# Layer norms: GpSimd centres and weights half of each row

## What is computed

```python
def layer_norm(x, g, b):
    xf = x.astype(jnp.float32)
    mu = jnp.mean(xf, -1, keepdims=True)
    var = jnp.mean(jnp.square(xf - mu), -1, keepdims=True)
    y = (xf - mu) * lax.rsqrt(var + LN_EPS)
    return (y * g.astype(jnp.float32) + b.astype(jnp.float32)).astype(x.dtype)
...
    for l in range(DEPTH):
        x = layer_norm(alpha * x + 0.5 * swiglu(x, ffn_w_gate[l, 0], ffn_w_up[l, 0], ffn_w_down[l, 0]),
                       ln_g[l, 0], ln_b[l, 0])
...
```

## Time and profile before

| | us |
|---|---|
| median of 3 runs | 1566.58 |
| the 3 runs, lowest to highest | 1566.1 to 1567.77 |
| span of the profiled execution | 1564.4 |
| TensorE busy | 1550.8 (99%) |
| VectorE busy | 1054.8 (67%) |
| ScalarE busy | 771.3 (49%) |
| GpSimd busy | 35.5 (2%) |

### The profile page before, as it was taken

One profiled execution on the slowest core, in us unless ns is written; L12 is line 12 of the kernel. 1 busy time (PEld: TensorE's weight loads), 2 busy tenths in 40 slices (PEclk: granted clock), 3 DMA queues, 4 the chain that ended last, 5 costly groups with the idle time before them and its releaser, 6 DMA issues.

```text
span 1564.4 us, 20746 instructions
## 1 busy us (share of the span) xinstructions
PE 1550.8 (99%) x8610; PEld 1340.2 (86%) x8610; DVE 1054.8 (67%) x1290; ACT 771.3 (49%) x917; POOL 35.5 (2%) x86
## 2 busy tenths in 40 slices
PE   9999999999999999999999999999999999999998
PEld 9888888899888888888898888888888898888886
DVE  7866657768675666655777665576555778965556
ACT  5735434567353444445455354455454465454543
POOL 2000000000000000000100000010000100000000
PEclk9999999999999999999999999999999999999999
DMA  9365554743565656556463665547555573375551
GB/s 282 123 216 188 189 190 160 242 162 109 176 205 192 195 174 217 188 191 194 161 216 126 219 191 192 192 148 242 190 189 191 160 211 100 130 242 189 189 189 52
DMA packets 198357, 285.98 MB, mean 183 GB/s; under 512 B 9199, under 2 KB 166967, under 8 KB 198263
## 3 DMA queue, kind: packets, MB, share of 16 engines
q1 hardware_dynamic: 194663, 272.19, 53.4%
q0 software_dynamic: 3456, 11.94, 2.3%
q10 hardware_dynamic: 144, 0.52, 0.1%
HBM read 283.58 MB, written 1.05 MB: 182 GB/s over the span
## 4 chain that ended last, share of the span: by engine, by line
PE 95%; DVE 3%; ACT 1%; issue 1%; DMA 0%; DVEq 0%; ACTq 0%
PE ps L438 50%; PE ps L467 25%; PE ps L471 13%; PE ps L490 3%; DVE wlo L299 1%; PE ps L1652 1%; PE ps L1964 0%; ACT whi L288 0%; PE ps L1456 0%; DVE arena L2174 0%; PE ps L1644 0%; DMA x<-in_x 0%; DVE small L940 0%; DVE x L566 0%; PE ps L1131 0%
## 5 line engine op out<-in xcount | busy, mean ns | idle before, releaser
L299 DVE TENSOR_TENSOR wlo<-raw,whi 128x2048 fp32r<-128x2048 f32 (+3 forms) x254 | 567.0, 2262 | 219.8 <-ACT whi L288 219.1
L288 ACT ACTIVATE whi<-raw 128x2048 fp32r<-128x2048 f32 (+3 forms) x260 | 479.8, 1882 | 18.9 <-DMA raw<-in_w_out 4.9
L438 PE MATMUL ps<-whi,yt 128*128 128x512 f32 (+1 forms) x1472 | 460.9, 386 | 0.5 <-DVE wlo L299 0.5
L467 PE MATMUL ps<-xt,whi 128*128 128x512 f32 x1728 | 432.4, 392 | 0.0
L467 PEld LDWEIGHTS ps<-xt,whi 128*128 128x128 f32 x1728 | 314.1, 189 | 59.1
L438 PEld LDWEIGHTS ps<-whi,yt 128*128 128x128 f32 x1472 | 274.8, 188 | 54.8 <-DVE wlo L299 0.9
L438 PE MATMUL ps<-wlo,yt 128*128 128x512 f32 (+1 forms) x736 | 283.7, 385 | 0.0
L471 PEld LDWEIGHTS ps<-xt,wlo 128*128 128x128 f32 x1728 | 235.7, 190 | 16.9
L471 PE MATMUL ps<-xt,wlo 128*128 128x256 f32 x1728 | 240.9, 282 | 0.0
L438 PE MATMUL ps<-whi,xt 128*128 128x512 f32 (+4 forms) x778 | 219.0, 359 | 0.8 <-issue 0.3
L777 ACT ACTIVATE arena<-ps 128x512 f32<-128x512 f32 x108 | 64.1, 593 | 280.5 <-PE ps L471 280.5
(11 more groups left out here) (242 smaller groups left out, 958.6 us busy)
## 6 DMA issues: line engine op xcount, KB each, us to landing
raw<-in_ffn_w_up SPq DMA_DIRECT2D x76, 1024.0 KB, 5.3
raw<-in_ffn_w_down SPq DMA_DIRECT2D x76, 1024.0 KB, 4.9
raw<-in_ffn_w_gate SPq DMA_DIRECT2D x44, 1024.0 KB, 5.3
raw<-in_diff_w_qkv SPq DMA_DIRECT2D x12, 1024.0 KB, 5.0
raw<-in_w_in_conv SPq DMA_DIRECT2D x10, 1024.0 KB, 5.0
raw<-in_w_out SPq DMA_DIRECT2D x8, 1024.0 KB, 4.9
raw<-in_w_in_mlstm SPq DMA_DIRECT2D x7, 1024.0 KB, 8.0
raw<-in_w_in_mlstm SPq DMA_DIRECT2D x8, 768.0 KB, 4.2
```

The source lines that it names most:

```text
L288: nc.scalar.activation(whi[:, u.slot, 0:u.size], raw[:, u.slot, 0:u.size], ACT.Copy).then_inc(w_hi[u.slot], 1)
L299: nc.vector.tensor_tensor(wlo[:, u.slot, 0:u.size], raw[:, u.slot, 0:u.size], whi[:, u.slot, 0:u.size].bitcast(F32), ALU.subtract).then_in ...
L438: m = nc.tensor.matmul(out_, p, q, start=first and n == 0, stop=last and n == 2, skip_group_check=True)
L467: nc.tensor.matmul(o.rearrange("p (a n) -> p a n", a=2), parts[c][0], xt2[:, :, c, :], start=c == 0, stop=False, skip_group_check=True)
```

## The change

In each norm and row tile, GpSimd now does the centring of columns 512 to 1023 in two instructions: `tensor_scalar` subtracts the mean (it waits for `ln_var`), and `tensor_tensor` multiplies by the gain (it waits for the first, by a new semaphore `ln_centred`). VectorE keeps the centring of columns 0 to 511, the root and both scalings; ahead of the second scaling it waits for `ln_centred`. GpSimd's loop over the norms now also covers norm 9, without a load behind it.

```diff
@@ ln_normal (VectorE)
-            def centre(h):
-                half = slice(h * 512, h * 512 + 512)
-                link.mark(nc.vector.scalar_tensor_tensor(
-                    out=res[:, t, half], in0=res[:, t, half], scalar=mv[:, t, 0:1],
-                    in1=gb[:, 0, half], op0=ALU.subtract, op1=ALU.mult))
+            half = slice(0, 512)
...
-            centre(0)
+            link.mark(nc.vector.scalar_tensor_tensor(
+                out=res[:, t, half], in0=res[:, t, half], scalar=mv[:, t, 0:1],
+                in1=gb[:, 0, half], op0=ALU.subtract, op1=ALU.mult))
             dve.wait_ge(ln_sd, TT * n + t + 1)
...
             scale(0)
-            centre(1)
+            dve.wait_ge(ln_centred, 2 * (TT * n + t) + 2)
             scale(1)
@@ ln_gpsimd
-            pool.wait_ge(ln_x, 4 * (n + 1))
-            load_gb(pool, n + 1)
+            half = slice(512, 1024)
+            for t in range(TT):
+                if t == 0:
+                    pool.wait_ge(gb_loaded, 32 * (n + 1))
+                pool.wait_ge(ln_var, TT * n + t + 1)
+                nc.gpsimd.tensor_scalar(res[:, t, half], res[:, t, half], mv[:, t, 0:1], None,
+                                        ALU.subtract).then_inc(ln_centred, 1)
+                pool.wait_ge(ln_centred, 2 * (TT * n + t) + 1)
+                nc.gpsimd.tensor_tensor(res[:, t, half], res[:, t, half], gb[:, 0, half],
+                                        ALU.mult).then_inc(ln_centred, 1)
+            if n < N_LN - 1:
+                pool.wait_ge(ln_x, 4 * (n + 1))
+                load_gb(pool, n + 1)
```

More of the change, by code:

```diff
@@ L374, in build @@
         ln_sd = sem("ln_sd")
+        ln_centred = sem("ln_centred")
         sd = sb("sd", [P, TT])
@@ L2545, in _ @@
                 .then_inc(mem_loaded, 16)
-            for n in range(N_LN - 1):
+            for n in range(N_LN):
                 for f in ffns:
-                    if f.gated and FFN_LN[f.k] + 1 == n:
+                    if f.gated and FFN_LN[f.k] + 1 == n < N_LN - 1:
                         split_lo_gpsimd(pool, order[f.tail[0].index + 4])
```

## The result

The changed kernel takes 1573.68 us (median of 5 runs, 1573.4 to 1575.31), the kernel before 1566.55 (median of 5, 1566.1 to 1567.77). The ratio is 1.0048, with a 95% interval of 1.0038 to 1.0059: 7.1 us slower, where 10 were forecast.

A forecast was written before the change was run, and what follows sets the result against it. TensorE was taken as the bound, waiting on VectorE's scalings. Delays of 8.7 (first scalings), 0.6 (norms 7 and 9) and 0.9 (first row tiles) sum to 10.2 us, giving 1577 from 1566.6; range 1568 to 1585.

The forecast's parts named there:

- the forecast case: Whole kernel: GpSimd's multiplication holds the first scaling, making the time 1574 to 1580 us; chance 0.45.
- The main mechanism: In each norm, GpSimd's multiplication takes the shared ports ahead of the first scaling, which ends 1.09 us late.
- the first scaling keeps its 0.75 us: Sign that the prediction is wrong: the first scaling's row stays at 0.75 us instead of reading 1.4 to 1.7.
- the second of the prediction's steps: Length of GpSimd's subtraction of the mean: 0.50 us after the centring, ending 1.24 after the centring's start.
- The next step: GpSimd's multiplication takes the ports at about 1.54 us after the centring's start and keeps them 1.12, until 2.66.
- the first scaling wins the race: Rival: the first scaling gets the ports before GpSimd's multiplication; +1 to +4 us, 1568 to 1570; chance 0.17.
- The rival of a slower GpSimd: GpSimd's subtraction takes 1.12 us instead of 0.50, 8 us more, 1590; chance 0.27 together with small instructions held.
- 8 x 1.09 = 8.7: Second row tile of norms 0 to 6 and 8: TensorE waits 1.09 us longer for the first scaling, 8.7 us.
- 5 x 0.31 = 1.5: Second scaling 0.31 us late in five places: norms 7 and 9, and first row tiles of norms 4, 6, 8.
- The rival of no collision: VectorE and GpSimd overlap on these operands; the second scaling starts earlier, -1.4 us, 1565.2; chance 0.08.
- the second rival: VectorE's small instructions (L573, L575) are held by GpSimd too; 1582 us; chance 0.27 together with a slower GpSimd.
- The estimate from the Trainium skill's GPSIMD Engine Reference (§3.1): GpSimd's one-input loop of 512 elements priced at 768 ns, 0.27 us more per place, 3.5 us more, 1580.

The follow-up runs named there:

- run 1: The kernel before, with 22 scratch instructions for GpSimd alone (subtractions and multiplications) between 40 and 80 us; 1569.06 us in its only timed run.
- Run 10: The changed kernel with GpSimd's subtraction over 64 columns instead of 512, the multiplication still over 512; 1574.02 us.
- run 9: The changed kernel with the second row tile put back on VectorE, GpSimd doing the first row tile alone; 1568.35 us.
- run 3: The changed kernel without GpSimd's subtraction and its wait, so that GpSimd only multiplies; 1574.04 us.
- run 5: The changed kernel with VectorE's centring of columns 0 to 511 taking its second tensor from PSUM, not the gain from SBUF; 1570.18 us.
- run 6: The changed kernel with L572 and L574 written as operations of one tensor and two per-row numbers; 1574.10 us.
- run 4: The changed kernel without GpSimd's multiplication, so that GpSimd only subtracts; 1567.47 us.
- run 7: The changed kernel with GpSimd on columns 768 to 1023 alone, VectorE centring 512 to 767 between its two scalings; 1567.93 us.
- run 2: The changed kernel with a constant, 0.25, in place of the mean in GpSimd's subtraction; 1572.66 us.
- run 8: The changed kernel with GpSimd released by the mean and not by the variance, 0.25 us earlier; 1573.03 us.

## Why the prediction was right, and where it was not

The direction and the place held. TensorE is the bound, what counts most is the two scalings of the second row tile, and shared ports put GpSimd behind the centring. The time lay 3.3 us under the point and inside the range, just below the forecast case (1574 to 1580).

The main mechanism did not hold. The prediction named its own sign of being wrong, that "the first scaling keeps its 0.75 us", and it does. Of its other signs, L593 ended 1.44 us after the centring and not 0.5, and VectorE's idle for `ln_centred` is 1.22 us and not near zero. The waits of L490 did grow to "13 or more" (13.8), but not by 1.4 each: they are more waits, for both scalings. That the time still came out near the forecast is in part luck, as the sum below shows.

The step that failed is the length of GpSimd's subtraction, the second of the prediction's steps: "It ends at 1.24. As bounds I take 0.50 and 1.12". The subtraction ended at 2.18, 1.44 after the centring. The row used, a selection over 512 columns (`sel` in the earlier trace rows), is a different operation, and on 4 partitions; run 1 measured 1.56 us for this one. The upper bound, 1.12, was a two-input instruction's time, and run 1 shows that the one-input instruction takes longer, 1.56 against 1.27. What the estimate of 0.50 did describe is how long it holds the ports: L572 ended at 1.31, forecast "about 1.3".

The next step fell with it: "it takes the ports at about 1.24 + 0.3 = 1.54". The multiplication was issued at 2.26, after the first scaling had begun at 1.61. So the rival "the first scaling wins the race" is what happened, but not by the race of 0.1 to 0.3 us that I described, and not at its price. It gave 0.2 to 0.4 for the second scaling; the chain that is 0.9 longer makes it 0.76. Run 10, with a shorter subtraction, shows the collision that was forecast, at 1574, where it was priced at 1577: its scalings ended 2.97 and about 3.6 after the start, where 3.21 and 3.88 were forecast. The rival of a slower GpSimd had a longer subtraction add 8 us more (1590). It takes the collision with the first scaling away instead: with 512 columns the time is 1573.7, with 64 it is 1574.0.

The terms of the sum: 8 x 1.09 = 8.7 for the first scaling became 8 places of 0.49 on average, 3.9, paid for the second scaling less what TensorE had to spare. The 5 x 0.31 = 1.5 for the second scaling in norms 7 and 9 and in the first row tiles of 4, 6 and 8 became 0.77 + 0.7 + 2.1 = 3.6. The five places were the right ones (run 9: 2.1 us for the three first row tiles). So a term that was 4.8 too high and one that was 2.1 too low partly cancelled, which is luck.

The rival of no collision (-1.4) is excluded by runs 3 and 5. The small instructions are held too, as the second rival supposed: 0.24 us in the changed kernel, 0.84 in run 3. It was L572 that was hit, by the subtraction, and that cost nothing (run 6).

The rule of the Trainium skill (SBUF — State Buffer, "Who interferes with whom") speaks of the whole instruction. Run 3 agrees for the multiplication (L572 ended 0.02 after it); for the subtraction the measurement differs, since L572 and most of the first scaling (its first 0.57 us of 0.75) ran while it was still under way. The estimate from the Trainium skill's GPSIMD Engine Reference (§3.1), 768 ns, lay nearer than 0.50 and was still half of what was measured.

No run is faster than the kernel before; runs 4 and 7 show why. By the prediction's reading the gain to be had is 0.7 us in two places, and in each variant here GpSimd's instructions hold, or are held by, one of the two scalings or a centring.

## What to carry to other kernels

Moving half of an engine's work to an idle engine can pay only if the new chain, with its hand-overs, ends before the old one would have, and holds nothing on the path meanwhile: here 0.74 us of VectorE's time became 1.56 + 1.27 us on GpSimd, without collisions. Take the price of an instruction from a row of the same operation or measure it alone; a row of a like one missed by a factor of three. And ask of a shared port how long each side holds it: in every row here a VectorE instruction with two SBUF inputs and a GpSimd instruction with two finish one behind the other, and dividing such work between the two engines gained nothing at 256 columns (run 7) and lost at 512.

## What was not expected of the hardware

- GpSimd's subtraction of one number for each row takes 1.56 us over 512 columns, its multiplication of two tensors 1.27; over 256 columns 0.92.
- The one-input instruction lets VectorE go well before its end. L572 ends 0.57 us after the centring, the subtraction over 512 columns 1.44 after it; over 256 columns (run 7) it is 0.35 and 0.79. The two-input one holds VectorE to its end (run 3).
- GpSimd's multiplication also holds a VectorE instruction with one tensor in SBUF, L991 in run 1: 1.44 us in place of 0.35.
- With the number in SBUF the subtraction seems to come to the ports twice. The one at 46.87 in run 1 began under a split of VectorE that ended at 48.04, did not delay the next (2.28 us), and ended 1.35 after that one. With a constant, L572 is held 0.09 us less (run 2). That the first visit is for the number is inferred from these two, not shown.
- When GpSimd's subtraction started 0.01 us ahead of the centring (run 8, second row tiles), the centring still took its 0.74 us. L573, the small instruction, then took 0.37 us, as with the constant, and the subtraction ended 0.09 earlier than in the changed kernel. That would fit a first visit made ahead of the centring; it is not shown either.
- At the start of the changed kernel's execution GpSimd's `sel`, which took 0.63 us in the earlier trace rows, took 1.45, beside a split that began 0.01 us earlier; it ends 0.50 after it. Timeline of GpSimd, then VectorE:

```profile
10.13 1.45 POOL L2388 TENSOR_SCALAR_AFFINE_SELECT sel<-sel 4x512 f32<-4x512 f32 x1
...
10.12 0.96 DVE L325 TENSOR_TENSOR wlo<-raw,whi 128x768 fp32r<-128x768 f32 x1 [0.35 <-ACT whi L317]
```
